# Products at the ends of two stages, nine fill pieces in place of six, one wait split in the feed-forward loops, and the coarsest recurrent level as a 64 by 64 product

## The reference, cut to what matters

```
# block 1, state space head: y = sum over taps of the state response + d_skip * u; gelu
# blocks 1 and 2, feed-forward: up-projection, a convolution over tokens,
#   silu(gate) * val (block 1) or gelu(conv(val)) * gate (block 2), down-projection
# block 2: proj = modulate(x) @ w_in_2, columns for a gated recurrence, a short
#   convolution and a spatial gate
def step(s, inp):                      # gated recurrence, per head and direction
    b = jnp.cumsum(gc, axis=2)
    inter = jnp.einsum('bhtk,bhkv->bhtv', qc * jnp.exp(b), s)
    diff = b[:, :, :, None, :] - b[:, :, None, :, :]
    decay = jnp.where(causal, jnp.exp(jnp.minimum(diff, 0.0)), 0.0)
    scores = jnp.einsum('bhtk,bhtsk,bhsk->bhts', qc, decay, kc)
```

## Time and profile before

| what | value |
|---|---|
| median of 3 runs | 2635.65 us (2635.13 to 2636.76) |
| the profiled execution | 2637.23 us, span 2635.5 us |
| PE busy | 2492.3 us, 95% of the span |
| DVE busy | 1621.6 us, 62% |
| ACT busy | 885.9 us, 34% |
| mean granted PE clock | 0.984 |

### The profile page before, as it was taken

The page is one execution under the profiler, slowest core; times in us unless marked ns, Lnnn a source line. Parts: engine busy times, 40 slices in busy tenths (PEclk is TensorE's granted clock), DMA queues, the critical chain, the costliest instruction groups (busy, mean ns, idle before and its releaser), DMA issues. The chain is left out here.

```text
span 2635.5 us, 39178 instructions
## 1 busy us (share of the span) xinstructions
PE 2492.3 (95%) x16559; PEld 1344.0 (51%) x16737; DVE 1621.6 (62%) x2109; ACT 885.9 (34%) x1057; POOL 26.8 (1%) x60
## 2 busy tenths in 40 slices
PE   7989798999999999999899999989979999999997
PEld 3457564444444444443567777764434444444443
DVE  6688747544444443655458878786766666774253
ACT  5117307333232231323344545452332222222121
POOL 0000000020000000000000000000000000000000
PEclk9989899999999999999999999999989999999998
DMA  9027464111121124343100000022101112113432
GB/s 326 27 77 238 148 223 144 33 32 48 55 57 48 48 60 125 105 115 131 53 25 25 25 24 18 25 81 64 33 16 48 48 48 63 49 54 104 110 108 88
DMA packets 302918, 207.37 MB, mean 79 GB/s; under 512 B 11296, under 2 KB 298174, under 8 KB 302143
## 3 DMA queue, kind: packets, MB, share of 16 engines
q1 hardware_dynamic: 301910, 205.08, 26.0%
q10 hardware_dynamic: 873, 0.32, 0.0%
HBM read 191.22 MB, written 13.64 MB: 78 GB/s over the span
## 5 line engine op out<-in xcount | busy, mean ns | idle before, releaser
L200 PE MATMUL ps<-hT,arena 128*128 128x512 bf16 (+1 forms) x6114 | 1330.0, 377 | 35.7 <-DVE arena L2090 9.9
L200 PEld LDWEIGHTS ps<-hT,arena 128*128 128x128 bf16 x6240 | 609.7, 98 | 756.7 <-issue 35.7
L1911 PE MATMUL ps<-arena 128*128 128x512 bf16 x2068 | 455.8, 379 | 5.4 <-DVE arena L1893 3.2
L1911 PEld LDWEIGHTS ps<-arena 128*128 128x128 bf16 x2112 | 206.4, 98 | 252.0 <-DVE arena L1893 5.1
L2163 DVE SCALAR_TENSOR_TENSOR arena<-ps,vec,arena 128x945 f32<-128x945 f32 (+2 forms) x176 | 215.1, 1222 | 75.6 <-ACT arena L2149 56.3
L2130 DVE SCALAR_TENSOR_TENSOR arena<-ps,vec,arena 128x1023 f32<-128x1023 f32 (+1 forms) x88 | 106.8, 1276 | 182.5 <-ACT arena L2120 182.5
L1893 DVE TENSOR_TENSOR arena<-hT,arena 128x2816 bf16<-128x2816 f32 (+2 forms) x44 | 93.7, 2157 | 163.7 <-ACT arena L1887 163.6
L1887 ACT ACTIVATE arena<-hT 128x2816 bf16<-128x2816 f32 (+2 forms) x44 | 77.8, 1798 | 239.6 <-DMA hT<-w_down_dram 112.3
L2953 PE MATMUL ps<-arena 128*128 128x128 f32 x896 | 109.8, 279 | 11.7 <-DVE arena L3268 11.6
L2077 DVE TENSOR_TENSOR arena<-hT,arena 128x2048 bf16<-128x2048 f32 x44 | 100.9, 2292 | 28.2 <-ACT arena L2044 27.9
L2953 PEld LDWEIGHTS ps<-arena 128*128 128x128 f32 x896 | 105.2, 194 | 15.5 <-DVE arena L3268 14.4
(11 more groups left out here) (421 smaller groups left out, 2473.1 us busy)
## 6 DMA issues: line engine op xcount, KB each, us to landing
xT<-ada_w_dram SPq DMA_DIRECT2D x24, 1024.0 KB, 5.4
hT<-w_up_dram SPq DMA_DIRECT2D x44, 512.0 KB, 5.0
hT<-ffn_up_dram SPq DMA_DIRECT2D x44, 512.0 KB, 4.9
hT<-w_down_dram SPq DMA_DIRECT2D x30, 704.0 KB, 7.0
hT<-ffn_down_dram SPq DMA_DIRECT2D x30, 704.0 KB, 6.9
arena<-w_in_dram SPq DMA_DIRECT2D x33, 512.0 KB, 4.0
xT<-w_mod_dram SPq DMA_DIRECT2D x16, 1024.0 KB, 5.4
arena<-w_mod_dram SPq DMA_DIRECT2D x8, 1024.0 KB, 19.4
```

What stands on the lines that cost most here:

```text
L200: last = pe.matmul(out, lhs(a, kt), rhs(b, kt, i), start=start and kt == 0 and (a, b) == (0, 0), stop=stop and kt == n_k - 1 and (a, b) == ...
L1911: last = pe.matmul(self.bank(u), self.part(u, a, kt), self.g[:, b, kt, cols], start=kt == 0 and (a, b) == (0, 0), stop=kt == FT - 1 and (a ...
```

## The change

It has five parts. In `stage_ssm` the kernel products signal tile by tile, lie in the upper columns of four other PSUM banks, start after the first of the two loops of powers, and follow the late pieces in place of preceding them; `within(0)` waits for tile 0 alone. In `Ffn.pe_rest` the wait for `done[b]` becomes one for `conved[b]` ahead of the value part and one for `g_hi[b]` ahead of the gate part. At the end of the short-convolution stage one more weight tile is loaded before the last down-projection unit, and PE does the gate products of blocks 0 and 1 there; at the end of `stage_spatial_gate` PE does the first front of the recurrence (48 matmuls), for which the transposes move to other banks. In `stage_hgrn` the three late gate tiles are filled in nine pieces, one after each unit, the last in the middle of the last unit. And level 0 multiplies 64 by 64.

```diff
@@ -1539,7 +1539,7 @@
-    kern_ps = k.ps[:, 4:6, :].rearrange("p b (q d n) -> p (b q) d n", q=2, n=H2)
+    kern_ps = k.ps[:, 0:4, 2 * STEPS:4 * STEPS].rearrange("p q (d n) -> p q d n", n=H2)
@@ -1617,6 +1617,7 @@
             chunk_states(0)
+            late.pe(pe, range(LATE_ATT + 2, LATE_ATT + 4))
             pe.wait_ge(w_ready, 1)
@@ -1626,10 +1627,9 @@
-            last.then_inc(kern_made, 1)
-            late.pe(pe, range(LATE_ATT + 2, LATE_ATT + 4))
-            pe.wait_ge(kern_ready, U_TILES)
+                last.then_inc(kern_made, 1)
             for q in range(U_TILES):
+                pe.wait_ge(kern_ready, q + 1)
                 within(q)
                 late.pe(pe, late_at(q, 1, 2))
@@ -1655,11 +1655,12 @@
-            act.wait_ge(kern_made, 1)
-            for r in range(SPU):
-                rows = slice(H2 * r, H2 * r + H2)
-                act.activation(kern[rows, :, :, rows], kern_ps[rows], ACT.Copy).then_inc(kern_taken, 1)
-            act.wait_ge(w_ready, 1)
+            for first, end in ((0, 1), (1, U_TILES)):
+                act.wait_ge(kern_made, end)
+                for r in range(SPU):
+                    rows = slice(H2 * r, H2 * r + H2)
+                    act.activation(kern[rows, first:end, :, rows], kern_ps[rows, first:end], ACT.Copy).then_inc(kern_taken, 1)
+            act.wait_ge(w_ready, 2)
             attn.act_squares(act, (0,))
@@ -1687,17 +1688,22 @@
-            dve.sem_inc(w_ready, 1)
-
-            dve.wait_ge(kern_made, 1)
+                dve.sem_inc(w_ready, 1)
+
+            late.dve(dve, range(LATE_ATT + 2, LATE_ATT + 4))
+            def with_skip(q):
+                stt(kern[:, q, 0, :], k.ident[:, :], k.col("ssm_d", q), kern[:, q, 0, :], ALU.mult, ALU.add).then_inc(kern_ready, 1)
+
+            dve.wait_ge(kern_taken, SPU)
+            with_skip(0)
+            dve.wait_ge(kern_made, U_TILES)
             link(dve.tensor_copy(decay, params.s(params.MAG).unsqueeze(2).to_broadcast((P, N, STEPS))))
             link(dve.memset(decay[:, :, 0:1], 0.0))
             dve.wait_ge(c_taken, 8)
             link(dve.memset(st[:, :, :, 0:1], 0.0))
-            dve.wait_ge(kern_taken, SPU)
-            for q in range(U_TILES):
-                stt(kern[:, q, 0, :], k.ident[:, :], k.col("ssm_d", q), kern[:, q, 0, :], ALU.mult, ALU.add).then_inc(kern_ready, 1)
-            late.dve(dve, range(LATE_ATT + 2, LATE_ATT + 4))
+            dve.wait_ge(kern_taken, 2 * SPU)
+            for q in range(1, U_TILES):
+                with_skip(q)
@@ -1950,7 +1956,7 @@
-        at = [None] + [i * 2 * KD * P for i in (0, 1, 3)]
+        at = [None, F_S, 2 * KD * P, 6 * KD * P]
@@ -2031,9 +2037,10 @@
         with pe.Fori(1, FT // 2) as i:
             for b in range(2):
                 pe.wait_ge(self.lo[b], i + 1 + b)
-                pe.wait_ge(self.done[b], i + 1)
                 for half in range(2):
                     for s in range(2):
+                        if half == 0:
+                            pe.wait_ge(*((self.conved[b], i) if s == 0 else (self.g_hi[b], 2 * i - 1)))
                         last = self.part(pe, b, half, s)
                 last.then_inc(self.made[b], 1)
@@ -2181,11 +2188,12 @@
+EARLY_VALUES = 2
 
 
 def gate_weights(k):
 
-    return (k.ar(F_S, KD, GATE_COLS),
+    return (k.ar(F_S + 2 * KD * P, KD, GATE_COLS),
@@ -2261,8 +2269,10 @@
             short.load(sp, 0)
+            sp.wait_ge(down.made, last_u)
+            short.load(sp, 1)
             sp.wait_ge(down.made, 2 * KD)
-            for n in range(1, len(parts)):
+            for n in range(2, len(parts)):
                 short.load(sp, n)
@@ -2352,6 +2362,10 @@
                 short_unit(n, 1, (lambda kt: m_norm.wait_parts(pe, 1, kt)) if n == 0 else None).then_inc(made, 1)
+            pe.wait_ge(gate_lo, 1)
+            pe.wait_ge(copied, 1)
+            for b in range(EARLY_VALUES):
+                gate_values(k, pe, gate_parts, b)
@@ -2428,12 +2442,11 @@
-            short.hi(act, 0)
-            short.hi(act, 1)
+            for n in range(3):
+                short.hi(act, n)
             squares = m_norm.steps((1,))
             for i, n, a, b, t in squares[:4]:
                 m_norm.act_square(act, i, a, b, t)
-            short.hi(act, 2)
             for i, n, a, b, t in squares[4:]:
                 m_norm.act_square(act, i, a, b, t)
             short.hi(act, 3)
@@ -2549,6 +2562,7 @@
                 if u == last_u:
                     short.lo(dve, 0)
+                    short.lo(dve, 1)
@@ -2565,17 +2579,16 @@
             centre_tiles(steps[:4])
-            short.lo(dve, 1)
+            short.lo(dve, 2)
             m_norm.dve_add(dve, i, a, b, t)
-            short.lo(dve, 2)
             short.lo(dve, 3)
             m_norm.dve_finish(dve, (1,))
             dve.wait_ge(gate_hi, 1)
-            dve.tensor_tensor(gate_parts[:, 1], gate_raw, gate_parts[:, 0], ALU.subtract)
+            dve.tensor_tensor(gate_parts[:, 1], gate_raw, gate_parts[:, 0], ALU.subtract).then_inc(gate_lo, 1)
@@ -2606,6 +2619,20 @@
+def gate_values(k, pe, parts, b):
+
+    return split_matmuls(pe, [k.ps[:, b // 2, (b % 2) * SG_WIDTH:(b % 2 + 1) * SG_WIDTH]],
+                         lambda s, kt: k.hT[:, s, kt, CTX + b * P:CTX + (b + 1) * P],
+                         lambda s, kt, i: parts[:, s, kt, P:GATE_COLS], KD)
+
+
+def first_front(k, pe, stream):
+
+    stream.ready(pe, 0)
+    split_matmuls(pe, [k.ps[:, half, :] for half in range(2)], lambda s, kt: stream.part(0, s, kt),
+                  lambda s, kt, half: k.hT[:, s, kt, half * HALF:(half + 1) * HALF], KD)
@@ -2681,10 +2708,8 @@
-            for b in range(nb):
-                last = split_matmuls(pe, [k.ps[:, b // 2, (b % 2) * SG_WIDTH:(b % 2 + 1) * SG_WIDTH]],
-                                     lambda s, kt: k.hT[:, s, kt, CTX + b * P:CTX + (b + 1) * P],
-                                     lambda s, kt, i: parts[:, s, kt, P:GATE_COLS], KD)
+            for b in range(EARLY_VALUES, nb):
+                last = gate_values(k, pe, parts, b)
                 if b % HB == HB - 1:
                     last.then_inc(v_made, 1)
@@ -2713,9 +2738,10 @@
                     for b in range(HB):
-                        last = pe.transpose(k.ps[:, 2 * t + i, b * P:(b + 1) * P],
+                        last = pe.transpose(k.ps[:, 4 + 2 * i + t, b * P:(b + 1) * P],
                                             rows_mixed[:, HB * i + b, t * P:(t + 1) * P], k.ident[:, :])
                     last.then_inc(turned, 1)
+            first_front(k, pe, stream)
@@ -2847,16 +2873,18 @@
-    FILL = {-1: (0, 0, T), 0: (1, 0, HALF), 1: (1, HALF, HALF + CTX), 2: (2, 0, HALF), 4: (2, HALF, T), 6: (1, HALF + CTX, T)}
+    FILL = {-1: (0, 0, T), 0: (1, 0, 3 * P), 1: (1, 3 * P, 4 * P), 2: (1, 4 * P, 7 * P), 3: (1, 7 * P, T),
+            4: (2, 0, 3 * P), 5: (2, 3 * P, 4 * P), 6: (2, 4 * P, 6 * P), 7: (2, 6 * P, T)}
...
-                [(n, "level", 2), (n, "level", 3)] + front_of_next(V0) + [(n, "level", 4)] + \
+                [(n, "level", 2), (n, "level", 3)] + ([(n, "fill", 0)] if n == last_unit else []) + \
+                front_of_next(V0) + [(n, "level", 4)] + \
                 front_of_next(GATE, V1, QUERY) + [(n, "level", l) for l in range(5, NL)] + \
-                ([(n, "fill", 0)] if n in FILL else [])
+                ([(n, "fill", 0)] if n in FILL and n < last_unit else [])
     jobs.append((last_unit + 1, "ss", 0))
@@ -2950,8 +2978,16 @@
-                chunk_job((n, "level", l), range(T // P), lambda out, c: pe.matmul(
-                    out, v[:, c * P:(c + 1) * P], v[:, c * P:(c + 1) * P], start=True, stop=True))
+                d, m = units[n][1], LEVELS[l]
+                whole = 2 * m < P
+                rows = slice(0, P) if whole else slice(d * m, (d + 1) * m)
+                columns = slice(0, P) if whole else slice((1 - d) * m, (2 - d) * m)
+
+                def product(out, c):
+                    chunk = v[:, c * P:(c + 1) * P]
+                    return pe.matmul(out[rows, columns], chunk[:, rows], chunk[:, columns], start=True, stop=True)
+
+                chunk_job((n, "level", l), range(T // P), product)
@@ -2974,7 +3010,8 @@
-            for piece in PIECES[0]:
+            pe.sem_inc(made[0], 1)
+            for piece in (Z1, V0, V1, QUERY):
                 front(0, piece)
             fill(-1)
@@ -3000,6 +3037,8 @@
                 level(n, 3)
+                if n == last_unit:
+                    fill(n)
                 pe.wait_ge(states_ready, n + 1)
@@ -3014,7 +3053,8 @@
                     level(n, l)
-                fill(n)
+                if n < last_unit:
+                    fill(n)
                 pe.wait_ge(selected, n + 1)
@@ -3154,8 +3194,8 @@
-                    act.wait_ge(late_gates.filled, len(FILL))
-                    for i in range(4):
+                    act.wait_ge(late_gates.filled, 5)
+                    for i in range(2):
@@ -3173,7 +3213,8 @@
```

(16 more changed lines are left out.)

## The result

The changed kernel takes **2598.82 us** (median of 4 runs, 2597.6 to 2603.25), the kernel before 2636.2 in the same comparison (2635.13 to 2640.69): a ratio of 0.9858, 95% interval 0.9841 to 0.9875. The profiled execution took 2599.3 us. The prediction said 2601, within 2592 to 2613.

The account below looks back on a forecast made before the run. The prediction took PE, busy 95% of the span, as the bound, so only its waits or work count. Eight terms summed to -34.3 us; against the median of 2635.65 that gave 2601.4, stated as 2601, within 2592 to 2613.

Parts of the forecast that it names:

- Part 1: State space stage: earlier kernel products and `within(0)` remove 9.0 us of wait and one low-clock stretch, -11.8 us.
- Parts 2 and 3: Feed-forward loop starts: -4.5 us in block 1, -3.5 in block 2; added waits taken as free, bound +6.
- Parts 4 and 5: Short convolution's weight waits and first border together -11.9 us; second border -3.2 us.
- Part 6: Gate-tile fills spread over recurrence units 0 to 6: -4.1 us, bounds -0.5 and -5.
- Part 7: Level 0 at 64 by 64: 0 us, since DVE decides when level 1 starts; bound -7.2.
- Rival B: Shorter level 0 counts because DVE is ready by its end: 7.2 us come off, 2594; chance 0.09.
- Part 8: Last recurrence unit: its fill holds up DVE and costs +4.7 us, bounds +2.6 and +5.6.
- Rival A: Clock falls in the recurrence's units behind longer idles ahead of level 1: +8 to +14 us, about 2612; chance 0.12.
- C: Borders and first stage give less: DVE binds the state space stage, 3.1 us of clock stays lost; 2611; chance 0.13.
- D: Slower: mid-turn waits in the feed-forward loops stop PE loading weights ahead; 2642 at 1 us each; chance 0.02.
- E: No effect: each removed wait is replaced by the next one at the same time, about 2634; chance 0.02.

Follow-up runs that it names:

- c2: The kernel before with only level 0 changed, to 64 by 64; 2638.08 us against 2635.98, ratio 1.0005.
- b5: The changed kernel with the old state space stage, but its two late pieces moved ahead of the kernel products; 2608.99 us, ratio 0.9895.
- a4: The changed kernel with the state space stage of the kernel before; 2614.24 us.
- b2: The changed kernel with the feed-forward loops' old single wait in place of the two new ones; 2607.94 us.
- b1: The changed kernel with both borders as before: all eight gate blocks behind the first, the recurrence's first projection behind the second; 2612.22 us.
- a2: The changed kernel with level 0 at 128 by 128 again; 2602.17 us.
- c3: The changed kernel with level 0 at 128 by 128 again, repeated for a second profile; 2600.34 us.
- a3: The changed kernel with DVE weighing level 1 ahead of evacuating the diagonal in units 0, 2, 4 and 6; 2602.58 us.

## Why the prediction was right

**The sum.** -34.3 predicted, -37.9 measured between the profiles. 1.5 of the difference lies ahead of the change and is chance; 2.4 is part 1. The others are each within 0.7 us, and their errors cancel, which is in part luck: so do larger ones inside parts 3 and 6.

**Part 1** is the term that was mis-sized: -11.8 against -14.2. Its wait was right: 9.0 predicted, 9.3 measured, and 3.0 of clock at `within(0)` came back. But "products from 286.4, 5.2 us long as they are" was wrong: they started when I said (284.89 with the 1.5 us from ahead) and took 3.66. That bought little, since `within(0)` then waited 1.28 us for the skip of tile 0. Missing from the sum was the block at 328.65, 6.11 us long, which I had not looked at. Three groups ran cold, and the clock is 1.6 + 3.0 + 2.6 = 7.2 us of PE's time, of which the 1.6 went mostly into that wait. I had counted one cold group only. The third is partly chance: it was cold in two of the three profiles of the old stage (6.11 and 6.06 us), while c2 lost 1.4 at a later group instead, and b5 was warm there. So the term was short by 1.4 to 2.7 us (c2 13.2, a4 14.5).

**Parts 2 and 3**: the waits as worked out, down to the 3.4 us that remain in block 2; the bound of +6 for the added waits was not needed (b2). The low clock that I left behind those 3.4 us is there in nine of the eleven profiles that have the idle; in the first it had gone to the norm's sums, so that -3.9 is close to -3.5 with 1.7 us lost at one place and more than that won at the other. **Parts 4 and 5**: the trace gives -4.8 for the weights, -6.6 for the first border and -3.1 for the second, where 5.0, 6.9 and 3.2 stood. b1 shows that the work moved into the idle is the cause at both borders; for the weights no run shows it. **Part 6**: right in sum (-4.65 for -4.1) but not unit by unit. From the end of one unit's transposed keys to that of the next it is -1.3 in units 0, 2 and 4 (-0.85 each predicted), none in unit 1 (-0.5), +0.5 in unit 3 (none), and -1.3 in unit 5 (-1.0), where the idle of 1.98 us is 0.66 now and the cold product behind it is gone.

**Part 7**: right, and shown three times (a2, c3, c2). The 0.8 us that each level 0 saves (1.15 us is 0.59 of 1.95, not the half that I had taken) became idle, 0.48 or 0.73 to 1.38 or 1.44. Rival B falls. In one point the forecast missed: in the odd units level 1 starts 4.86 us behind the diagonal product (1375.29 to 1380.15), not 4.53, since PE reaches the diagonal earlier against DVE there; in the even units, and in c2, the distance is the old one. a3 says more: with DVE's order changed, ACT's exponential is next in line, so that level 1 came 0.95 us sooner in unit 0 and only 0.4 in unit 2.

**Part 8**: right in place (DVE stands at the fill for 5.19 us, predicted 5), +5.3 for +4.7. The cold fill that five of the profiles show adds 1.1 to 1.4.

**Rival A** was half right. It asked for a cold level 1 in each unit; 6 of 80 are cold. After the same 1.38 us the clock holds or falls. The Trainium skill (TensorE: Matmul & The Clock Gate, A second HAM failure mode: psum-queue depth-cycling) says that frequent short idles between groups of matmuls let the clock oscillate; the traces agree in 6 blocks of 80, which is 0.9 us a run where the rival had 8 to 14. **C, D and E** didn't happen: the borders gave what they should, and D's waits cost nothing.

## What to carry to other kernels

Halving the work of the bounding engine gives nothing where another engine sets the next start: look for the wait that ends last there, and follow it one engine further before reordering it. A filler belongs in the stretch where its engine is idle now, and its evacuation must not stand ahead of what the other engines wait for; moving one filler ahead of two levels gave back 4.5 to 5.3 us. When you price a removed idle, look at all the matmul groups near it that ran at the lower clock, not only the next one, and in more than one profile: part of them are cold by chance.

## What the hardware showed that I had not expected

The same instructions behind the same idle get either clock level: level 1 after 1.38 us took 2.05 or 3.52 us, levels 2 and 3 after 3.07 took 6.67, after 3.06 in two other runs 2.02 and 2.05, or 3.10 and 2.54. In block 2 the loss falls either on the norm's sums (8.80 us for 7.10) or on the start of the loop some 40 us later. The idle of 5.2 us ahead of level 3, by contrast, was followed by a cold block in all eleven profiles that have it (3.60 to 3.79 us for 2.05). And the late pieces moved into a wait (b5) did not warm what came behind it: 6.50 us for products that took 5.21 with the pieces after them, in one profile.
